# A two-layer mixer network on TensorE: modulation work spread through the pair loop, one low half made by VectorE

## The reference

```python
shift, scale, gate = split(silu(c) @ w_mod[i] + b_mod[i], 3)
h = rmsnorm(x, norm_g[i]) * (1 + scale) + shift
# layer 0                               # layer 1
z, bg, cg, xh = split(h @ a_w_in, 4)    z, u, v = split(h @ b_w_in, 3); u, v = gelu(u), gelu(v)
y = conv3(cg * xh) * bg * silu(z)       y = u * (w_s @ layernorm(v) + b_s) * silu(z)
x = x + gate * (y @ w_out)
```

## Time and profile before

| what | value |
|---|---|
| median of 3 runs (lowest, highest) | 854.31 us (854.06, 856.63) |
| the profiled execution: its own time | 856.63 us |
| its span in the profile | 854.8 us |
| busy: PE, DVE, ACT, POOL | 97%, 72%, 46%, 10% |
| last chain: PE, DVE, DMA | 85%, 8%, 4% |

### The profile page before, as it was taken

One profiled execution on the slowest core, in us unless ns is written; L12 is line 12 of the kernel. 1 busy time (PEld: TensorE's weight loads), 2 busy tenths in 40 slices (PEclk: granted clock), 3 DMA queues, 4 the chain that ended last, 5 costly groups with the idle time before them and its releaser, 6 DMA issues.

```text
span 854.8 us, 14184 instructions
## 1 busy us (share of the span) xinstructions
PE 825.3 (97%) x5026; PEld 741.8 (87%) x5026; DVE 612.7 (72%) x940; ACT 395.6 (46%) x542; POOL 88.9 (10%) x84
## 2 busy tenths in 40 slices
PE   5897999999999999999999999999999999998996
PEld 5676999999999999987889888888888888887896
DVE  5989688888878888788872755577776666758334
ACT  4346566766666666653222842244344443412210
POOL 2511122222222222100000100000000000000000
PEclk9899899999999999999989999999999999999999
DMA  7675789798888888678641143322222222066102
GB/s 273 222 252 142 158 177 207 187 218 185 197 182 198 184 200 183 180 290 308 236 154 40 62 146 98 98 78 95 98 76 95 74 98 78 20 226 229 63 1 99
DMA packets 50252, 130.48 MB, mean 153 GB/s; under 512 B 4272, under 2 KB 20784, under 8 KB 50224
## 3 DMA queue, kind: packets, MB, share of 16 engines
q1 hardware_dynamic: 31120, 107.05, 36.1%
q0 software_dynamic: 18816, 22.02, 17.2%
q10 hardware_dynamic: 288, 1.05, 0.3%
HBM read 105.99 MB, written 2.10 MB: 126 GB/s over the span
## 4 chain that ended last, share of the span: by engine, by line
PE 85%; DVE 8%; DMA 4%; issue 1%; ACT 1%; SPq 1%; DVEq 0%; ACTq 0%
PE pp L749 13%; PE pp L750 12%; PE pp L751 12%; PE pp L881 7%; PE pp L882 7%; PE pp L883 7%; PE p_aux L881 4%; PE p_aux L882 4%; PE p_aux L883 4%; PE pp L1024 3%; PE pp L1025 3%; PE pp L1026 3%; DVE acc_s L1151 3%; DMA raw<-in_stream 2%; PE p_aux L1077 1%
## 5 line engine op out<-in xcount | busy, mean ns | idle before, releaser
L455 ACT ACTIVATE w_hi<-raw 128x1024 fp32r<-128x1024 f32 x77 | 81.5, 1059 | 189.3 <-PE pp L751 122.5
L1131 DVE TENSOR_TENSOR w_lo<-raw,w_hi 128x1024 fp32r<-128x1024 f32 x80 | 97.4, 1222 | 68.3 <-ACT w_hi L455 67.9
L749 PE MATMUL pp<-y_hi,w_hi 128*128 128x512 f32 (+1 forms) x320 | 113.9, 356 | 2.7 <-DVE x L1517 2.7
L750 PE MATMUL pp<-y_lo,w_hi 128*128 128x512 f32 (+1 forms) x320 | 112.5, 352 | 0.0
L751 PE MATMUL pp<-y_hi,w_lo 128*128 128x512 f32 (+1 forms) x320 | 112.4, 351 | 0.0
L749 PE MATMUL pp<-h_hi,w_hi 128*128 128x512 f32 x256 | 100.1, 391 | 0.0
L751 PE MATMUL pp<-h_hi,w_lo 128*128 128x512 f32 x256 | 99.7, 389 | 0.0
L750 PE MATMUL pp<-h_lo,w_hi 128*128 128x512 f32 x256 | 99.6, 389 | 0.0
L881 PE MATMUL pp<-h_hi,wh 128*128 128x256 f32 x280 | 79.4, 283 | 0.0
L882 PE MATMUL pp<-h_lo,wh 128*128 128x256 f32 x280 | 79.4, 283 | 0.0
L883 PE MATMUL pp<-h_hi,wl 128*128 128x256 f32 x280 | 79.3, 283 | 0.0
(11 more groups left out here) (188 smaller groups left out, 1953.3 us busy)
## 6 DMA issues: line engine op xcount, KB each, us to landing
raw<-in_stream SPq DMA_DIRECT2D x160, 512.0 KB, 4.3
wl<-raw POOLq DMA_DIRECT2D x28, 512.0 KB, 4.6
raw_l<-in_stream SPq DMA_DIRECT2D x25, 512.0 KB, 4.6
wl<-raw POOLq DMA_DIRECT2D x28, 256.0 KB, 4.9
raw_m<-in_stream SPq DMA_DIRECT2D x7, 512.0 KB, 4.2
x_s<-in_xt SPq DMA_DIRECT2D x4, 512.0 KB, 6.4
x<-in_xt SPq DMA_DIRECT2D x4, 512.0 KB, 5.8
out_t<-x SPq DMA_DIRECT2D x8, 256.0 KB, 2.3
```

The costliest lines, as they stand in the source:

```text
L455: act.activation(to[:, slot[0], :], raw[:, slot[1], :], ACT.Copy).then_inc(hi_cut, 1)
L749: pe.matmul(out, hi, rhs_hi(kt), start=first and n == 0, stop=False)
L750: pe.matmul(out, hi, rhs_lo(kt), start=False, stop=False)
L1131: dve.tensor_tensor(lo[:, slot[0], :], raw[:, slot[1], :], f32(hi[:, slot[0], :]), ALU.subtract).then_inc(consumed, 1)
```

## The change

It does five things. (1) Every pair step does both halves of a modulation group, not one; 14 halves are done in the loop, 10 (not 17) in layer 0's output product, and layer 1's eight are spread over three j. (2) The column products are put one by one ahead of a group of three matmuls in the two units of s = 3: eight in each of j = 0, 1, 2 of layer 0, and 2, 4, 2 in layer 1. (3) Q5 and Q2 wait for the first y for odd g alone. (4) The low half of B11 is a VectorE subtraction behind `t_sums` (`b11_low`); ScalarE's negative and GpSimd's DMA for it are gone. (5) The order changes in three places: VectorE's last low half of the activation sums (`s_low(3)`) goes behind the first y, SyncE loads one output slot ahead of layer 1's late halves and the others between them by a new count, and the biases are added in fewer, larger pieces.

```diff
-LOOP_MODS = {1: 10, 2: 12, 3: 14, 4: 16, 5: 18, 6: 13, 7: 15}
-AOUT_MODS = [[(8, 0), (8, 1), (12, 1)], [(9, 0), (9, 1), (14, 1), (16, 1), (18, 1), (13, 1)],
-             [(10, 1), (15, 1), (17, 0), (17, 1), (19, 0), (19, 1)], [(11, 0), (11, 1)]]
-BOUT_MODS = [[(20, 0), (20, 1), (21, 0), (21, 1)], [(22, 0), (22, 1), (23, 0), (23, 1)]]
+LOOP_MODS = {1: 10, 2: 12, 3: 14, 4: 16, 5: 18, 6: 8, 7: 9}
+AOUT_MODS = [[(13, 0), (13, 1)], [(15, 0), (15, 1), (17, 0), (17, 1)], [(19, 0), (19, 1), (11, 0), (11, 1)], []]
+BOUT_MODS = [[(20, 0), (20, 1)], [(21, 0), (21, 1), (22, 0), (22, 1)], [(23, 0), (23, 1)]]
+COLUMNS = [[[8, 9, 10, 12], [14, 16, 18, 13], [15, 17, 19, 11]], [[20], [21, 22], [23]]]
...
 # SyncE
-                    if g == 3 and i < PAIRS - 1:
-                        sp.wait_ge(m_used, i)
-                        load_mod(i + 1)
+                    if g == 3:
+                        load_mod(i, 1)
+                    if g == 5:
+                        load_mod(i + 1, 0)
...
+            load_late(done + 1)
             sp.wait_ge(blocks, FREE + 2 * W_BOUT)
             for n in range(4):
                 load_late_mod(1, n)
-            n = 4
-            for w in range(done + 1, W_END):
-                load_late(w)
-                if w > done + 1 and n < len(late_mods(1)):
-                    load_late_mod(1, n)
-                    n += 1
+            for j in range(DPAIRS):
+                for s in range(4):
+                    w = done + 2 + 4 * j + s
+                    if w < W_END:
+                        load_late(w)
+                    for _ in range(len((BOUT_MODS + [[]])[j][2 * s:2 * s + 2])):
+                        n += 1
+                        load_late_mod(1, n)
...
 # GpSimd, in the pair loop
-                            pool.wait_ge(neg, of_pair(i, g, 2, 1))
-                            pool.sem_inc(lo_begun, 1)
-                            pool.dma_start(wl[par][:, B_11:N_W].bitcast(F32).rearrange("p (k e) -> p k e", e=P),
-                                           raw[:, 2 * par, :].rearrange("p (k u e) -> p k u e", u=2, e=P)[:, :, 0, :],
-                                           accum_op=ALU.add).then_inc(b11_in[par], 16)
...
 # ScalarE, cut_b11
-                act.activation(hi, b11, ACT.Copy)
-                act.activation(lo, b11, ACT.Copy, scale=-1.0).then_inc(neg, 1)
+                act.activation(hi, b11, ACT.Copy).then_inc(b11_hi, 1)
...
 # TensorE, unit
                 for n, kt in enumerate(kts):
                     hi, lo = stationary(n)
+                    if beside is not None:
+                        beside(n)
...
+            def column(layer, j, n):
+                group, t = COLUMNS[layer][j][n // 2], n % 2
+                if n == 0:
+                    done = N_LOOP_MODS + layer * len(late_mods(0))
+                    pe.wait_ge(m_used, done + ((0, 2, 10), (2, 6, 8))[layer][j])
+                    pe.wait_ge(mod_read, ((0, 1, 1), (2, 3, 4))[layer][j])
+                at = 2 * (group - (8, 20)[layer]) + t
+                mm = pe.matmul(p_small[:, at:at + 1], group_acc(group)[:, P * t:P * (t + 1)], ones[:, 0:1],
+                               start=True, stop=True)
+                if n == 2 * len(COLUMNS[layer][j]) - 1:
+                    mm.then_inc(acc_used, 1)
...
 # q5 and q2
-                pe.wait_ge(y_made, 1)
+                if g % 2:
+                    pe.wait_ge(y_made, 1)
...
 # out_product
-                    if s == 3:
-                        gate_columns(layer, j)
...
+                        def beside(n):
+                            if s == 3 and 4 * u + n < 2 * len(COLUMNS[layer][j]):
+                                column(layer, j, 4 * u + n)
...
-            group_columns(range(12, 20), N_LOOP_MODS + sum(len(part) for part in AOUT_MODS[:3]), 3)
...
 # VectorE
+            def b11_low(i, g):
+                par = g % 2
+                dve.wait_ge(b11_hi, of_pair(i, g, 1, 1))
+                part = raw[:, 2 * par, :].rearrange("p (k u e) -> p u k e", u=2, e=P)[:, 0, :, :]
+                lo, hi = (a[par][:, B_11:N_W].rearrange("p (k e) -> p k e", e=P) for a in (wl, wh))
+                dve.tensor_tensor(lo, part, f32(hi), ALU.subtract).then_inc(b11_cut, 1)
...
                 t_sums(i, 2)
+                b11_low(i, 2)
                 c_12(i, 0)
-                if mods:
-                    loop_mod(i)
+                loop_mod(i, 0)
...
                     silu_mul(i, at[0])
+                    loop_mod(i, 1)
                     t_low(i, 4, 1)
...
-                add_bias(2 * KD + 2 * j, (16, 18), 5 + j)
                 if j == 0:
+                    add_bias(2 * KD, (0, 6), 5, 1)
                     dve.wait_ge(x_again, 64)
                 update_x(0, j)
```

81 lines of the change are left out of this document (38 added, 43 removed).

## The result

The changed kernel took 846.58 us in the median of four runs (845.46 to 847.38), the kernel before, on the same chip, 855.47 (854.06 to 859.01): a ratio of 0.989, 95% interval 0.985 to 0.993. The forecast was 846.6, range 843.5 to 851.0. The single number is nearer than the reasoning: the forecast was subtracted from a median of 854.31, while the drop itself was forecast at 7.7 us and measured at 8.9 here, and at 9.0 and 10.5 on two other chips further down. On the profiled execution, 848.9 was forecast and 845.46 measured.

The account below looks back on a forecast made before the run. TensorE, busy 825.3 of 854.8 us, was taken as the bound, so time could return from its waits, low clock and own work. Terms -1.6 + 0.6 - 1.7 - 2.8 + 0.2 + 0.5 - 2.9 = -7.7 from 854.31 gave 846.6, range 843.5 to 851.

Parts of the forecast that it names:

- start of the pair loop: First pair: Q5, Q6 and Q2 no longer wait for y, Q7 starts 3.8 us earlier, less 2.2 for low clock: -1.6.
- the loop: Pair loop steps: c_22(0) reaches TensorE with no slack, 0.1 us late in each of six crossings: +0.6.
- wait before s = 3: Layer 0's output product: the 2.1 us wait hangs on a modulation half's load; order and loads are kept: 0.
- clock in j = 0: Layer 0's output product, 387.5 to 391.5: without the column work behind the wait, the clock stays up: -1.7.
- block of 16: Layer 0's block of 16 modulation columns from 440.20: spreading them saves the time lost to the low clock: -2.8.
- other columns: The other 16 columns cost 3.67 us in five blocks and 3.84 alone: +0.2.
- new wait: Layer 0, j = 0: the last column comes late, so add_bias and the first update_x hold up TensorE once: +0.5.
- layer 1's output product: The 2.7 us wait goes: one slot is loaded ahead of the halves, VectorE does two halves in j = 0, not four: -2.9.
- the rival to which I gave 0.10: The clock does not fall at the pair loop's start: -2.2, giving 844.4 us; chance 0.10.
- I charge 2.2: Pair loop's start: the new 3.1 us gap drops the clock, costing 2.2 us; the old fall lost 2.6.
- Late crossings: Rival: in the pair loop the crossing is 0.5 us a step later than summed, +2.4, giving 849.0 us; chance 0.08.
- VectorE-bound loop: Rival: instruction order leaves VectorE idle, so pair-loop steps grow; with 4.5 us left idle, 857.9 us; chance 0.05.

Follow-up runs that it names:

- the blocks of eight: Changed kernel with each sweep's columns in one block ahead of the products of s = 3, not spread; median 849.03 us.
- the two experiments: Changed kernel with layer 1's first slot loaded behind the first four halves, 853.24 us; or with its eight halves split four and four, 850.46 us (medians).

## Why the prediction was right, and where it was not

Term by term, on the profiled executions, by the stages above:

| term | forecast | measured |
|---|---|---|
| start of the pair loop | -1.6 (-3.8 to -1.2) | -3.7 |
| the loop | +0.6 (0 to +1.5) | 0.0 |
| wait before s = 3, with the first slot's | 0 | -0.5 |
| clock in j = 0, block of 16, other columns, new wait | -1.7 - 2.8 + 0.2 + 0.5 = -3.8 | -1.4 - 2.4 = -3.8 |
| layer 1's output product | -2.9 (-3.1 to -1.5) | -3.4 |
| sum | -7.7 | -11.4 |

**Start.** The mechanism was right to 0.1 us (Q7 at 88.31 for 88.25, a wait of 2.8 for a gap of 3.1), and the clock was the open part: it held, so the other end came true (-3.9 from Q1 to Q7, +0.2 because Q1 itself began later). This is the rival to which I gave 0.10, and it held in seven of the nine profiled executions with this very wait. The two others show the fall, and it costs 1.45 to 1.5 us, not the 2.2 charged. The step that failed is "I charge 2.2": taken as certain, and from one fall of 6.8 us, while the three falls at the start that were seen since lasted 3.4. By the medians, undoing this part costs 1.3 us. The sentence on the watch that runs free of the program (the Trainium skill, TensorE: Matmul & The Clock Gate, What's actually happening) is what the repeated runs bear out: same code, same wait, with and without the fall.

**Loop.** `c_22(0)` started at 172.77 and its product at 173.35, the eighth (the second, Q5, at 164.71, plus 6 x 1.44); with 0.42 for the operation and 0.14 to TensorE it is on time to 0.02 us. VectorE in time:

```profile
161.84 2.04 DVE L1188 SCALAR_TENSOR_TENSOR acc_b<-raw_m,silu_c,acc_b 128x256 f32 x4
...
168.12 0.68 DVE L1341 TENSOR_TENSOR wl<-raw,wh 128x512 fp32r<-128x512 f32 x1
...
172.77 0.42 DVE L1359 TENSOR_TENSOR tmp<-p_aux,pc 128x256 f32<-128x256 f32 x1
```

"No slack at all" was right, "0.1 us late in each" was not, and the experiment shows how sharp the edge is: 0.6 us more there costs 0.59 a step. Late crossings and a VectorE-bound loop were rivals with good reason; VectorE was busy for 36.7 of 40 us, about 37.0 of a step's 40.3, a little below my 37.5. What I got wrong in words is that GpSimd's four DMAs "shorten no wait of TensorE". They shorten none of the waits of before. They would have made new ones: with them, the loop of the changed kernel is 2.3 us longer.

**Before s = 3.** Two effects, one foreseen. The first slot is late (0.36 behind y's low half, stage +0.5), and that comes out of the same wait, as forecast. The other, -0.46 on balance, I had put at 0 because "the change keeps that order and those loads": VectorE now idles 0.74 and 0.63 for the two halves' data, where it had idled 2.38 for one. Why they land sooner is open. Order is not arrival: with one and the same low half on VectorE, this stage took 17.4 to 17.8 us in most executions and 19.1 in one.

**Columns.** A lone column costs 0.23 us (0.24 forecast): from the column at 407.37 to the next at 408.28 it and three long matmuls take 0.91, of which the three are 0.68. The fall in j = 0 is gone, but not as forecast. I had taken it that the wait of 2.1 us stays and that the clock holds over it once the columns are spread. The wait was 1.0; with spread columns the clock held behind waits of 0.7 to 1.8 us in ten profiled executions, and fell in the one with 2.35. So the shorter wait, which I had not foreseen, may have had as large a part in the 1.7 us as the spreading. That the spreading matters at a wait of about 1 is what the blocks of eight show. The new wait is there: 0.33 behind x, gap 0.72 where 0.23 is the rhythm, 0.5 as summed. The size of a fall is not fixed: the same block of 16 was followed by 6.8 us at 1.2 GHz in one execution of before and by 3.4 in the experiment, 2.8 (the prediction's sum) or 1.4 us of time.

The Trainium skill (TensorE: Matmul & The Clock Gate, LDWEIGHTS (loading the stationary operand)) makes a weight load its columns over 1.2 GHz, 107 ns for 128, an estimated 0.21 for a lone column; the trace's 0.23 is near it, and nearer the 0.24 from the rows. In a block of 16 columns a pass follows the last by 0.11.

**Layer 1.** The wait went, and the two experiments show that undoing either part alone brings it back. Of the two reasons given, the slot was right; that VectorE does two halves fewer in j = 0 is not shown to matter by itself, since with four it still idles 5.2 us for that slot. The 3.4 us lie just outside the ends of the term: 2.9 are the wait with the slower first matmul, as summed, and 0.5 fell away around the blocks of columns and at the end, which this term did not cover.

The absolute number came out right to 0.02 us partly by luck: the median of three runs of before, 854.31, is low against the 855.5 to 857.2 of four other sets (the first of which has the same three runs and one more), and the drop is larger than 7.7 by 1 to 3 us. Between the two profiled executions the drop is 11.2 us, 3.5 more than the sum, and 2.1 of them stand at the loop's start.

## What to carry to other kernels

- Column work of one output element between long matmuls costs its passes and little more; the same passes in a block right behind a gap can cost more than twice as much through the clock (eight columns: 1.8 us, and 2.4 more). Spread them where a gap or a long block stands, and nowhere else is it worth the effort; and shorten the gap, since behind one of 2.35 us spread columns did not keep the clock.
- When two parts of a change share a queue, price them together. Here the part that seemed worth nothing (a low half on VectorE for one by DMA) saves 2.3 us in the loop (1.6 with what it costs at the start) of the kernel that also has the other (a second load in each step); before had that DMA and no late product. The same in layer 1: an edit of VectorE's shares was also an edit of a DMA queue, and acted through it.
- In an in-order engine, find the one hand-over without slack before counting free time. VectorE had over 3 us idle a step, and 0.6 us more cost 0.59 in one place and nothing 16 us earlier in the same step. The same search gave the last 3.9 us: three waits, each ended or shortened by moving an instruction past another that it did not need.

## What the hardware showed that I had not expected

- After one and the same idle stretch of 2.8 us TensorE's clock held in seven profiled executions and fell in two, each time 1.3 to 1.5 us after work had begun again, for 3.4 us. An idle stretch is a risk more than a price. Its length alone does not tell: in layer 1 the clock fell behind a wait of 2.06 us in one execution and held behind 2.52 and 2.7 in two others.
- Eight one-column matmul pairs in a row behind a gap of 1.26 us brought a fall of 6.8 us, though TensorE counts as busy throughout. The same eight behind gapless work brought none.
- A 256 KB adding DMA between tiles took 4.6 us at most times and 8.9 to 9.3 us in five of the seven steps, at a DMA share of 0.87; at 0.85, in the kernel before, the longest in the loop took 7.5 us, and no product waited for one.
- The time up to Q1, which no edit touches, varies by 1.7 us (79.3 to 81.0), with a clock of 0.76 to 0.84 in 20 to 40 us; a part of the spread of every kernel here is that.
